# An encoder block on one core: low parts of read-back activations made by GpSimd in place of VectorE

## The chip, the cores and the metric
One core of a Trainium2 chip runs the whole kernel. The metric is the device time in microseconds (us), the median of the runs. The engines are TensorE (PE: matmuls; PEld: its weight loads), VectorE (DVE), ScalarE (ACT), GpSimd (POOL) and SyncE (SP), which here only issues DMAs.

## The reference, cut to what matters
A bidirectional encoder block over 512 tokens with a model width of 2048, in float32: two attention branches merged by gates, then a SwiGLU feed-forward of inner width 5632, then a gated embedding, then a norm. The change lies at the switch inside the feed-forward:

```python
gu = rmsnorm(h, g_ffn[i]) @ w_gate_up[i]
g_, u_ = gu[..., :D_FF], gu[..., D_FF:]
h = h + (jax.nn.silu(g_) * u_) @ w_down[i]
```

## The kernel before, in words
**Precision.** A float32 matmul is made of three fp32r ones: each operand is split in a high part, its copy rounded to fp32r, and a low part, the operand minus the high part. The products are high x high, high x low and low x high. ScalarE makes the high parts, VectorE the low parts, for the weights as they stream in and for the activations.

**Units and products.** The feed-forward is a run of `UNITS` = 68 units, `FF` = 44 for gate and up and 24 for down, each a block of output rows that is computed with seven products in place of eight (a Strassen-Winograd scheme over halves of rows, columns and depth). Units go in pairs, and the products of the two units of a pair alternate: product `order(v, j)` = 14*(v//2) + 2*j + v%2, for j from 0 to 6, so there are 476, numbered 0 to 475. A product is `strassen(v, j)` on TensorE (lines 1197 to 1200 with the high part of the weights, line 1203 with the low part): 8 tiles of depth, 6 in the last generation. Weights of product n sit in slot `ring(n)` of three: ScalarE's `hi(n)` (line 1734, recorded as L1290) waits until TensorE has used product n-3, VectorE's `lo(n)` (line 2554) waits for `hi(n)`, TensorE waits for both. Four weight blocks of a unit (A11, A21, A22, A12) are loaded by SyncE in `block_load` (line 711) into slots of `RAWS`; the other operands of the seven products are sums of them: the first, A21 + A22, is an accumulating DMA that GpSimd issues, `sum_1(v)` (line 3009), after the loads of A21 and A22 of the unit; the others are subtractions of VectorE, `sum_2`, `sum_3`, `sum_4` (lines 2569, 2574, 2579). SyncE loads A22 of unit v after VectorE's `sum_4(v-2)` and `lo(order(v-2, 4))`, and A11 after `lo(order(v-2, 5))`.

**Generations of the down product.** Its activations are 22 row pairs; they are made in the gate-up stage, stored to DRAM (`hidden_store`), and read back as the second operand in three generations: units 44 to 51, 52 to 59 and 60 to 67. For a generation g of 1, 2, 3 there are seven operands x, blocks j = 0 to 6, held in the arena with a high and a low half. SyncE reads a block back with `fill(g, j)` (line 730) into the place of the low half, after TensorE has used the same slot of the generation before. Then each block is split in two parts h: ScalarE's `fill_split` rounds to the high half (L1290, arena<-arena), and `fill_low` (line 2561) subtracts it in place in the low half, 128x1024 values, 128x768 in generation 3. TensorE's first unit of a generation waits before product j for `fill_lo` to reach 14*(g-1) + 2*j + 2 (line 1184), so for both parts of block j.

**Where the fills stand.** `FILLS` (lines 445 to 462) hangs each part on a product number n; ScalarE does the split right after `hi(n)`, VectorE the low part right after `lo(n)`. For blocks 1 to 6 of a generation these are n = f + 10, 11, 13, 14, 16, 17, 19, 20, 22, 23, 25, 26 with f = 294, 350, 406, so 304 to 320, 360 to 376 and 416 to 432; the two parts of block 6 are needed by product f + 26 itself. Blocks 0 are filled ahead: at 170 and 226, at 352 and 353, at 408 and 409. In the same stretches VectorE adds the results of the units from PSUM into `res` (`add`, line 2742: `add_u3`, `add_c11_c12` and others), and up to unit 43 sums, scales and multiplies gate and up.

**Orders written out by hand.** Every engine's program is a fixed list with semaphore waits. On VectorE and ScalarE the loop over q (pairs of units) and t (0 to 13) does product 14*q + t + 2 and, beside it, what a table of `if`s says. GpSimd's list in this stage is `sum_1(v)` for all v and nothing else; it waits for loads most of the time. The first product of unit v waits on TensorE for `add_u3(v-2)`.

The functions that the diff touches and their callers:

Of the kernel before, what the change touches and what calls it, by code (L numbers as in the profile page):

```python
# [25 lines left out]
F32 = mybir.dt.float32  # L26
F32R = mybir.dt.float32r
ALU = mybir.AluOpType
# [52 lines left out]
UNITS = FF + 24  # L81
# [47 lines left out]
def raw_slot(v, i):  # L129

    if v < 2 and i == A12:
        return 8 + v
    return ((0, 7, 2, 4), (1, 5, 3, 6))[v % 2][(i - v // 2) % 4]


def raw_count(v, i):

    before = 0 if v < 2 and i == A12 else 16 * (Z_UNITS // 2)
    return before + (16 * (v // 2) if raw_slot(v, i) in (4, 6) else 16 if v < 2 else 16 * (v // 2 + 1))
# [39 lines left out]
def z_slot(v, i):  # L179

    return ((7, 4, 5, 2), (6, 0, 1, 3))[v % 2][(i - v // 2) % 4]
# [15 lines left out]
def build(nc, xT, pT, gains, tables, mats, w_in, w_z, w_qb, w_kvb, w_a, w_b, w_o, w_gu, w_dn, w_dn6, w_pg, w_pp,  # L197
          outT):
    with ExitStack() as ctx:
# [3 lines left out]
        def sem(name):  # L203
            return ctx.enter_context(nc.semaphore(name))
# [82 lines left out]
        fill_hi, fill_lo, added = sem("fill_hi"), sem("fill_lo"), sem("added")  # L287
# [25 lines left out]
        def sums(norm):  # L313
            return tab[:, 3, :] if norm == 4 else acc[:]
# [46 lines left out]
        def columns(v):  # L361
            return slice(0, pairs(v) * P)

        def ring(n):
            return (1, 0, 2)[n % 3]

        def operand(v, j):

            i = (A11, A21, A22, A12, A21, A12, A22)[j]
            return RAWS[raw_slot(v, i)][:, columns(v)]  # L370

        def x_slot(g, j):
            s, n = (7 * g + j) % 8, 6 if g == 3 else 8
            a = arena[:, 4 * s:4 * s + 4].rearrange("p u t c -> p (u t c)")
            return a[:, 0:n * 512].rearrange("p (t k c) -> p t k c", t=2, k=n)
# [83 lines left out]
        FILLS = {}  # L459
# [4 lines left out]
        def fill_part(g, j, h):  # L464
            n = 3 if g == 3 else 4
            return x_slot(g, j)[:, :, n * h:n * h + n]
# [1514 lines left out]
        def _(dve):  # L1981
            tt = nc.vector.tensor_tensor
# [78 lines left out]
            def head_square_lo(m):  # L2061
                dve.wait_ge(hsq_hi, m + 1)
                hi, lo = sq_parts(m)[:, 0:1, :], sq_parts(m)[:, 1:2, :]
                tt(lo, spare(m)[0], hi, ALU.subtract).then_inc(hsq_lo, 1)
# [252 lines left out]
            def seam_rotate(m, tile, before):  # L2317
                _, r, out = spare(m)
                dve.wait_ge(hnorm, m + 1)
                rotate(m, tile, 0, out, r, HD // 2, 2 * m + 2, before)  # L2320
                dve.wait_ge(roped, m + 1)
# [228 lines left out]
            def lo(n):  # L2550
                v, j = 2 * (n // 14) + n % 2, n % 14 // 2
                dve.wait_ge(s_hi, n + 1)
                s = ring(n)
                tt(S_LO[s][:, columns(v)], operand(v, j), S_HI[s][:, columns(v)], ALU.subtract).then_inc(s_lo, 1)  # L2554
                for part in FILLS.get(n, []):
                    fill_low(*part)

            def fill_low(g, j, h):
                dve.wait_ge(fill_hi, 14 * (g - 1) + 2 * j + h + 1)
                x = fill_part(g, j, h)  # L2560
                tt(x[:, 1], x[:, 1].bitcast(F32), x[:, 0], ALU.subtract).then_inc(fill_lo, 1)  # L2561

            def a_raw(v, i):
                return RAWS[raw_slot(v, i)][:, columns(v)]
# [27 lines left out]
            for g in range(8):  # L2592
# [16 lines left out]
                if g < 7:  # L2609
                    wlo(b + 4, 0)  # L2610
                else:
                    lo(0)
# [6 lines left out]
                if g == 7:  # L2619
                    x_low(14, T2_, SIX, res[:, 0:6, LEFT])  # L2620
                    x_low(15, B22_, SIX, res[:, 8:14, RIGHT])
                    lo(1)
                    x_low(16, T3_, SIX, res[:, 0:6, RIGHT])
# [349 lines left out]
        @block.gpsimd  # L2973
        def _(pool):
            def add_square(s, first, norm, sq):

                out = sums(norm)
                pool.wait_ge(sq_done, s + 1)
                if s == first:
                    if norm:  # L2980
                        pool.wait_ge(rstd_done, norm)
                    nc.gpsimd.tensor_copy(out, sq[:, s % 2, :]).then_inc(acc_done, 1)
                else:
                    pool.wait_ge(acc_done, s)
                    nc.gpsimd.tensor_tensor(out, out, sq[:, s % 2, :], ALU.add).then_inc(acc_done, 1)

            sq_a, sq_b = tmp[:, 2:4, :], tab[:, 0:2, :]
            for v in range(Z_UNITS):
                into, more = z_slot(v, A21), z_slot(v, A22)
                pool.wait_ge(s_in[into], 16 * (v // 2 + 1))  # L2990
                pool.wait_ge(s_in[more], 16 * (v // 2 + 1))
                pool.dma_start(RAWS[into], RAWS[more], accum_op=ALU.add).then_inc(sum_1_in[v % 2], 16)
            for norm, first, end in ((1, 16, 20), (2, 20, 24)):
                for s in range(first, end):
                    add_square(s, first, norm, sq_a)

            for p in range(8):
                pool.wait_ge(emptied, G_MERGE + p + 1)
                if p:
                    pool.wait_ge(mrg_lo, p)  # L3000
                else:
                    pool.wait_ge(gated_a_out[0], 16 * HEADS // 2)
                nc.gpsimd.tensor_tensor(tmp[:, 0:2, :], tmp[:, 2:4, :],
                                        res[:, GATE_IN[p % 2]:GATE_IN[p % 2] + 2, :], ALU.add).then_inc(mrg_sum, 1)
            def sum_1(v):
                into, more = raw_slot(v, A21), raw_slot(v, A22)
                pool.wait_ge(s_in[into], raw_count(v, A21))
                pool.wait_ge(s_in[more], raw_count(v, A22))
                pool.dma_start(RAWS[into][:, columns(v)], RAWS[more][:, columns(v)],  # L3009
                               accum_op=ALU.add).then_inc(sum_1_in[v % 2], 16)  # L3010

            for s in range(24, 38):
                add_square(s, 24, 3, sq_b)
            for v in range(UNITS):
                sum_1(v)
            for g in range(7):
                pool.wait_ge(pg_sig, g + 1)
                pool.wait_ge(emb_normed, 2 * g + 2)
                nc.gpsimd.tensor_tensor(tmp[:, 0:2, :], tmp[:, 0:2, :], emb[:, 2 * g:2 * g + 2, :],
                                        ALU.mult).then_inc(pg_mul, 1)  # L3020
                pool.wait_ge(pg_mul, g + 1)
                if g == 0:
                    pool.wait_ge(u_hi, 42)
                    pool.wait_ge(u_lo, 42)
                    pool.wait_ge(sq_done, 72)
                r = res[:, 2 * g:2 * g + 2, :]
                nc.gpsimd.tensor_tensor(r, r, tmp[:, 0:2, :], ALU.add).then_inc(pg_res, 1)
                for s in (72 + 2 * g, 73 + 2 * g):
                    add_square(s, 72, 6, sq_b)
# [117 lines left out]
```

## Time and profile before

| | us |
|---|---|
| median of 3 runs (2654.67 to 2655.56) | 2655.09 |
| the profiled execution's own time | 2658.29 |
| its span, first to last instruction | 2656.5 |
| TensorE matmuls busy | 2632.9 |
| VectorE busy | 2020.0 |
| ScalarE busy | 1286.2 |
| GpSimd busy | 179.1 |
| mean granted clock of TensorE, share of full speed | 0.998 |

"Busy" is the union of an engine's instructions; the matmuls are pipelined, so one of 256 columns is recorded with 0.28 us while the next starts 0.12 us later. Times in the trace are counted from the start of the span. The feed-forward runs from about 1125 to 2445 us.

### The profile page before, as it was taken

How to read it: one execution, taken by the hardware profiler on the slowest of the kernel's cores; microseconds unless marked ns; L12 is line 12 of the kernel's file. 1: busy time of each engine (PE TensorE's matmuls, PEld its weight loads, DVE VectorE, ACT ScalarE, POOL GpSimd, SP SyncE). 2: the span in 40 equal slices, each digit the busy share in tenths (PEclk: the TensorE clock that was granted, in tenths of full speed). 3: DMA queues.
4: the chain of work that ended last, by engine and by line, in shares of the span. 5: the costliest groups of instructions: out<-in, count | busy, mean ns of one | idle time of the engine just before them, and what ended most of it. 6: DMA issues, size and time to landing. Idle time of an engine off the chain costs nothing. (4 is left out here: it accounts for less than half of the span.)

```text
span 2656.5 us, 37937 instructions
## 1 busy us (share of the span) xinstructions
PE 2632.9 (99%) x14980; PEld 2309.0 (87%) x14980; DVE 2020.0 (76%) x2310; ACT 1286.2 (48%) x1612; POOL 179.1 (7%) x140
## 2 busy tenths in 40 slices
PE   9999999999999999999999999999999999999997
PEld 7989888888888888898888888888899898999887
DVE  7888767655565433488998999899899898888745
ACT  7545455434445233454554555554554453444543
POOL 0000000010000111100000000000000000000052
PEclk9999999999999999999999999999999999999999
DMA  7455323223333554446545555554666664643332
GB/s 247 139 160 163 127 87 95 79 88 112 107 94 108 182 208 124 146 126 180 165 143 177 172 153 167 175 151 151 177 210 216 190 224 126 208 137 106 94 103 96
DMA packets 137055, 392.75 MB, mean 148 GB/s; under 512 B 11584, under 2 KB 43456, under 8 KB 134336
## 3 DMA queue, kind: packets, MB, share of 16 engines
q1 hardware_dynamic: 121168, 342.27, 37.7%
q0 software_dynamic: 11232, 39.85, 8.5%
q10 hardware_dynamic: 4496, 8.44, 0.8%
q8 instruction: 109, 1.79, 0.3%
q14 instruction: 50, 0.41, 0.0%
HBM read 304.26 MB, written 46.40 MB: 132 GB/s over the span
## 5 line engine op out<-in xcount | busy, mean ns | idle before, releaser
L1290 ACT ACTIVATE w_hi<-raw 128x1024 fp32r<-128x1024 f32 (+1 forms) x539 | 563.3, 1046 | 756.8 <-PE ps L1203 408.3
L827 PE MATMUL ps<-arena,w_hi 128*128 128x512 f32 x2704 | 647.6, 391 | 1.3 <-DVE arena L2059 1.1
L827 PEld LDWEIGHTS ps<-arena,w_hi 128*128 128x128 f32 x2704 | 505.3, 188 | 109.9 <-issue 4.9
L1197 PE MATMUL ps<-arena,w_hi 128*128 128x512 f32 x1792 | 448.8, 392 | 0.5 <-DVE res L2742 0.5
L2554 DVE TENSOR_TENSOR w_lo<-raw,w_hi 128x1024 fp32r<-128x1024 f32 (+1 forms) x315 | 375.0, 1191 | 80.0 <-ACT w_hi L1290 78.3
L2005 DVE TENSOR_TENSOR w_lo<-raw,w_hi 128x1024 fp32r<-128x1024 f32 x172 | 219.3, 1275 | 233.3 <-ACT w_hi L1290 231.6
L1197 PEld LDWEIGHTS ps<-arena,w_hi 128*128 128x128 f32 x1792 | 322.3, 189 | 58.3 <-DVE res L2742 0.7
L1203 PEld LDWEIGHTS ps<-arena,w_lo 128*128 128x128 f32 x2468 | 332.3, 191 | 17.6
L1203 PE MATMUL ps<-arena,w_lo 128*128 128x256 f32 x2468 | 346.4, 282 | 0.0
L832 PE MATMUL ps<-arena,w_lo 128*128 128x512 f32 x1352 | 334.3, 389 | 0.0
L1290 ACT ACTIVATE hi<-raw 128x1024 fp32r<-128x1024 f32 (+1 forms) x183 | 190.4, 1041 | 250.8 <-PE ps L1203 208.2
L832 PEld LDWEIGHTS ps<-arena,w_lo 128*128 128x128 f32 x1352 | 253.8, 188 | 52.7
L1197 PE MATMUL ps<-arena,hi 128*128 128x512 f32 x896 | 224.4, 392 | 0.0
L2554 DVE TENSOR_TENSOR lo<-raw,hi 128x1024 fp32r<-128x1024 f32 (+1 forms) x157 | 187.1, 1192 | 46.7 <-ACT hi L1290 46.1
L1197 PEld LDWEIGHTS ps<-arena,hi 128*128 128x128 f32 x896 | 161.1, 189 | 28.8
L1203 PEld LDWEIGHTS ps<-arena,lo 128*128 128x128 f32 x1228 | 166.0, 191 | 8.7
L1203 PE MATMUL ps<-arena,lo 128*128 128x256 f32 x1228 | 172.9, 283 | 0.0
L1199 PE MATMUL ps<-arena,w_hi 128*128 128x256 f32 x676 | 166.9, 284 | 0.2 <-ACT res L1290 0.2
L1200 PE MATMUL ps<-arena,w_hi 128*128 128x256 f32 x676 | 166.7, 284 | 0.0
L3009 POOL DMA_DIRECT2D raw<-raw x68 | 59.1, 869 | 1224.0 <-DMA raw<-w_gu 785.8
L1199 PEld LDWEIGHTS ps<-arena,w_hi 128*128 128x128 f32 x676 | 130.3, 193 | 0.5 <-ACT res L1290 0.4
L1200 PEld LDWEIGHTS ps<-arena,w_hi 128*128 128x128 f32 x676 | 130.2, 193 | 0.1
(272 smaller groups left out, 3358.6 us busy)
## 6 DMA issues: line engine op xcount, KB each, us to landing
raw<-w_gu SPq DMA_DIRECT2D x174, 512.0 KB, 4.0
raw<-raw POOLq DMA_DIRECT2D x70, 512.0 KB, 7.9
raw<-w_in SPq DMA_DIRECT2D x68, 512.0 KB, 3.4
raw<-w_dn SPq DMA_DIRECT2D x64, 512.0 KB, 4.5
hid<-res SPq DMA_DIRECT2D x22, 1024.0 KB, 5.0
raw<-w_z SPq DMA_DIRECT2D x40, 512.0 KB, 5.0
raw<-w_o SPq DMA_DIRECT2D x32, 512.0 KB, 3.7
raw<-w_pg SPq DMA_DIRECT2D x32, 512.0 KB, 3.6
```

What stands on the lines that cost most here:

```text
L827: mm(ps[:, bank + t, :], w_hi[:, s, t, k], x[:, part, :], start=first and k == 0 and part == 0, stop=False)
L832: i = mm(ps[:, bank + t, :], w_lo[:, s, t, k], x[:, 0, :], start=False, stop=last and k == len(xs) - 1)
L1197: mm(parts, w, x[:, :, k], start=fresh and k == 0, stop=False, skip_group_check=not fresh)
L1199: mm(out, w, x[:, 0, k], start=fresh and k == 0, stop=False, skip_group_check=not fresh)
L1200: mm(out, w, x[:, 1, k], start=False, stop=False, skip_group_check=not fresh)
L1203: i = mm(out, lo[:, k * P:k * P + P], x[:, 0, k], start=False, stop=k == pairs(v) - 1, skip_group_check=not fresh)
L1290: return nc.scalar.activation(out, in_, ACT.Copy, scale=scale)
L2005: tt(w_lo[:, j % HL], raw[:, j], w_hi[:, j % HL], ALU.subtract).then_inc(w_lo_done, 1)
L2554: tt(S_LO[s][:, columns(v)], operand(v, j), S_HI[s][:, columns(v)], ALU.subtract).then_inc(s_lo, 1)
L3009: pool.dma_start(RAWS[into][:, columns(v)], RAWS[more][:, columns(v)], accum_op=ALU.add).then_inc(sum_1_in[v % 2], 16)
```

## The change
VectorE's `fill_low` and its call in `lo(n)` are taken out. The same function, with the same wait and the same semaphore, stands in GpSimd's program, and GpSimd's plain loop of `sum_1` becomes a loop over pairs of units in which the fills of products 14*q + 2 to 14*q + 15 stand around the two transfers of the next pair: places 2 to 9, then the even unit's transfer, place 10, the odd unit's transfer, places 11 to 15. `FILLS`, ScalarE, TensorE and SyncE are as before.

```diff
@@ VectorE
                 tt(S_LO[s][:, columns(v)], operand(v, j), S_HI[s][:, columns(v)], ALU.subtract).then_inc(s_lo, 1)
-                for part in FILLS.get(n, []):
-                    fill_low(*part)
-
-            def fill_low(g, j, h):
-                dve.wait_ge(fill_hi, 14 * (g - 1) + 2 * j + h + 1)
-                x = fill_part(g, j, h)
-                tt(x[:, 1], x[:, 1].bitcast(F32), x[:, 0], ALU.subtract).then_inc(fill_lo, 1)
@@ GpSimd
-            for v in range(UNITS):
-                sum_1(v)
+            def fill_low(g, j, h):
+                pool.wait_ge(fill_hi, 14 * (g - 1) + 2 * j + h + 1)
+                x = fill_part(g, j, h)
+                nc.gpsimd.tensor_tensor(x[:, 1], x[:, 1].bitcast(F32), x[:, 0], ALU.subtract).then_inc(fill_lo, 1)
+
+            def fill_lows(first, end):
+                for n in range(first, end):
+                    for part in FILLS.get(n, []):
+                        fill_low(*part)
+
+            sum_1(0)
+            sum_1(1)
+            for q in range(UNITS // 2):
+                fill_lows(14 * q + 2, 14 * q + 10)
+                if 2 * q + 2 < UNITS:
+                    sum_1(2 * q + 2)
+                fill_lows(14 * q + 10, 14 * q + 11)
+                if 2 * q + 3 < UNITS:
+                    sum_1(2 * q + 3)
+                fill_lows(14 * q + 11, 14 * q + 16)
```

## Rows read from the trace of the kernel before

**Rows 1.** Page, part 1: busy us, share of the span, instructions.
```profile
PE 2632.9 (99%) x14980; PEld 2309.0 (87%) x14980; DVE 2020.0 (76%) x2310; ACT 1286.2 (48%) x1612; POOL 179.1 (7%) x140
```

**Rows 2.** Waits of TensorE, whole span: us in total, times, longest.
```profile
PE ps L1199 <- DVE res L2742: 2.3, 1, 2.3
...
PE ps L1199 <- issue: 1.0, 1, 1.0
...
PE ps L1197 <- DVE res L2742: 0.5, 1, 0.5
```

**Rows 3.** Timeline of VectorE: products 317, 320 (its fill), 373, 429 (start, us).
```profile
2022.63 1.22 DVE L2554 TENSOR_TENSOR lo<-raw,hi 128x1024 fp32r<-128x1024 f32 x1
2023.76 1.22 DVE L2561 TENSOR_TENSOR arena<-arena 128x1024 fp32r<-128x1024 f32 x1
...
2031.58 1.22 DVE L2561 TENSOR_TENSOR arena<-arena 128x1024 fp32r<-128x1024 f32 x1
...
2182.85 1.22 DVE L2554 TENSOR_TENSOR w_lo<-raw,w_hi 128x1024 fp32r<-128x1024 f32 x1
...
2335.94 0.95 DVE L2554 TENSOR_TENSOR w_lo<-raw,w_hi 128x768 fp32r<-128x768 f32 x1
```

**Rows 4.** Timeline of TensorE: first matmuls of products 320, 376 and 432.
```profile
2032.90 0.36 PE L1199 MATMUL ps<-arena,hi 128*128 128x256 f32 x1 [1.02 <-issue]
...
2192.58 0.28 PE L1199 MATMUL ps<-arena,w_hi 128*128 128x256 f32 x1
...
2342.79 0.28 PE L1199 MATMUL ps<-arena,w_hi 128*128 128x256 f32 x1
```

**Rows 5.** Timeline of ScalarE and VectorE before TensorE's wait at 2349.5.
```profile
2346.31 0.84 ACT L1290 ACTIVATE hi<-raw 128x768 fp32r<-128x768 f32 x1 [4.57 <-DMA raw<-w_dn]
...
2348.07 1.41 DVE L2742 TENSOR_TENSOR res<-ps,res 128x512 f32<-128x512 f32 x2
```

**Rows 6.** Windows: length, busy (instructions) of PE, PEld, DVE, ACT, POOL; clock; DMA.
```profile
2350.00:2360.00 10.00, 10.00 (x74) 10.00 (x73) 7.40 (x11) 3.06 (x4) 0.00 (x0) 0.83 0.18 61
...
2360.00:2370.00 10.00, 10.00 (x86) 10.00 (x85) 9.69 (x13) 5.26 (x7) 0.00 (x0) 1.00 0.21 64
```

**Rows 7.** The same columns, three stretches with nine fills each.
```profile
1981.11:2022.63 41.52, 41.52 (x348) 41.44 (x347) 41.20 (x45) 26.64 (x30) 1.22 (x2) 1.00 0.76 262
2142.09:2182.85 40.76, 40.76 (x342) 40.76 (x341) 37.19 (x38) 24.20 (x24) 1.37 (x2) 1.00 0.64 214
2300.95:2335.94 34.99, 34.99 (x294) 34.99 (x293) 31.02 (x38) 19.81 (x24) 0.91 (x2) 1.00 0.57 179
```

**Rows 8.** Line 3003, GpSimd's additions ahead of w_o: ns min/median/max.
```profile
L3003 POOL TENSOR_TENSOR tmp<-tmp,res x8: 2391/2391/3300, 890.0 to 962.9; 128x1024 f32<-128x1024 f32 x8
```

**Rows 9.** Timeline of the tail, VectorE and GpSimd together.
```profile
2526.86 1.22 DVE L2017 TENSOR_TENSOR tmp<-ps,rstd 128x1024 f32<-128x1024 f32 x1
...
2527.55 1.30 POOL L2985 TENSOR_TENSOR acc<-acc,tab 128x512 f32<-128x512 f32 x1
...
2530.21 2.41 POOL L3019 TENSOR_TENSOR tmp<-tmp,emb 128x1024 f32<-128x1024 f32 x1 [1.35 <-DVE emb L2891]
2531.15 2.54 DVE L2005 TENSOR_TENSOR w_lo<-raw,w_hi 128x1024 fp32r<-128x1024 f32 x1 [1.09 <-ACT w_hi L1290]
2532.70 3.25 POOL L3027 TENSOR_TENSOR res<-res,tmp 128x1024 f32<-128x1024 f32 x1
```

**Rows 10.** Windows, VectorE's instructions on tile ps, first two stretches: busy (instructions), clock, DMA.
```profile
1981.11:2022.63 41.52, 4.77 (x8) 1.00 0.76 262
2142.09:2182.85 40.76, 5.70 (x10) 1.00 0.64 214
```

**Rows 11.** Timeline of GpSimd: accumulating transfers of units 47, 55 and 63.
```profile
2030.34 0.87 POOL L3009 DMA_DIRECT2D raw<-raw  x1 [6.26 <-DMA raw<-w_dn]
...
2189.20 0.86 POOL L3009 DMA_DIRECT2D raw<-raw  x1 [4.28 <-DMA raw<-w_dn]
...
2340.87 0.86 POOL L3009 DMA_DIRECT2D raw<-raw  x1 [2.78 <-DMA raw<-w_dn]
```

## The prediction, made before the change was run

> **What bounds the kernel now.** I read the busy times first: TensorE's matmuls cover 99% of the span of 2656.5 us, VectorE is at 76%, GpSimd at 7% [rows 1]. So nothing gets faster unless TensorE waits less, and anything gets slower that makes it wait. The chain of waits, TensorE's own part, comes next: in the stage of the edit (the switches between the gate-up product and the three generations of the down product) it waits three times: 1.0 us at 2032.9, 0.5 us a little later, and 2.3 us at 2349.5 [rows 2]. The 1.0 us is named "issue", but VectorE's low fill, the very instruction that moves, runs from 2031.58 for 1.22 us and TensorE goes on at 2032.90 [rows 3, 4]: it is the last fill of generation 1 that ends the wait. The 2.3 us end with an addition of VectorE that stood behind a weight block whose load was waited for 4.57 us [rows 5]; that load is issued once VectorE has made a low part, so a late VectorE is behind that wait too. After it the granted clock is 0.83 over ten microseconds, between the levels 2.4 and 1.2 GHz, and 74 matmuls start in place of about 86 (the stretch after it) [rows 6]: 12 x 0.12 us, 1.4 us more. The whole stake of the faster side is thus 1.0 + 0.5 + 2.3 + 1.4 = 5.2 us, 0.2% of the time.
>
> Why VectorE is late there is seen in three stretches, each from the first of a generation's fills to the start of the low part of the tenth product of the generation's first fourteen (317, 373, 429): it is busy 41.20 of 41.52, 37.19 of 40.76 and 31.02 of 34.99 us [rows 7], with nine fills in each. The relief is aimed at the right engine.
>
> **What is removed.** 42 subtractions on VectorE, 28 of 1024 columns and 14 of 768. In a back-to-back row one takes 1.13 us of its time (2022.63 to 2023.76) [rows 3]; for 768 columns I take 3/4 of that, 0.85. Two of the 42 (generation 1, block 0) and the four of blocks 0 of the others lie where VectorE has gaps: I cost them at nothing: the cover is those gaps and the ring of three slots that lets the low parts run ahead of TensorE; without it each would cost the 1.3 us by which the new hold is longer.
>
> **What is added.** The same subtraction on GpSimd. No row shows it in fp32r; the nearest is GpSimd's addition of 128x1024 f32 from two SBUF tiles, 2.39 us at least and in the middle, 3.30 at most [rows 8]. I take 2.39 us (1.8 for 768 columns, 3/4), upper bound 3.30; the lower bound is VectorE's own 1.13, since a rounding output could not make it faster than the faster engine.
>
> The decisive price is another. In the tail both engines work on SBUF at once, and there they don't share: GpSimd's multiply starts 2530.21 and takes 2.41, to 2532.62; VectorE's low part, normally 1.22, starts at 2531.15 and takes 2.54, to 2533.69, which is GpSimd's end plus 1.07. GpSimd's next addition, begun at 2532.70, then takes 3.25 in place of 2.39 [rows 9]. One waits for the other to end. An instruction of VectorE with an input in PSUM passes freely: L2017 (from ps and rstd) takes its 1.22 us at 2526.86, and GpSimd's addition that begins under it its 1.30 [rows 9]. The Trainium skill says the same and speaks against this change (SBUF — State Buffer, "Who interferes with whom": a VectorE instruction with two SBUF inputs and a GpSimd one that reads SBUF exclude each other for a whole instruction, while one SBUF input is free); by that rule moving a fill takes 2.39 us from VectorE in place of 1.13, not zero, and the trace agrees with its 2.54 us.
>
> So each move costs VectorE time. Nine fills per stretch: 9 x 2.39 = 21.5 us blocked, 9 x 1.13 = 10.2 us freed, +11.3 (generation 3: 16.2 - 7.7 = +8.5). Off that goes work that passes freely, VectorE's instructions on PSUM, 4.77 and 5.70 us [rows 10] and as much again in the third,, of which I take half since they come up at any point of a hold, and VectorE's idle time, 0.3, 3.6 and 4.0 us [rows 7]. VectorE reaches products 317, 373 and 429 later by
> 11.3 - 2.4 - 0.3 = 8.6; 11.3 - 2.85 - 3.6 = 4.9; 8.5 - 2.85 - 4.0 = 1.7 us.
>
> **The queue of GpSimd.** It is in order. The fills of its places 11 and 12 (block 6, both halves) stand behind the accumulating transfer of the odd unit, and this one waits for a weight block whose load SyncE issues only after VectorE's low part of product 317 (373, 429). From the start of that low part to the transfer's issue it is 2030.34 - 2022.63 = 7.7, 2189.20 - 2182.85 = 6.35 and 2340.87 - 2335.94 = 4.9 us [rows 3, 11]. The issue takes 0.87; then come two fills, 4.8 us (3.6), and 0.1 us to TensorE, which needs both for product 320 (376, 432). It would start it at
> 2022.63 + 8.6 + 7.7 + 0.9 + 4.8 + 0.1 = 2044.7, against 2032.90 [rows 4]: +11.8, less the 0.5 us wait right after it, +11.3;
> 2182.85 + 4.9 + 6.35 + 0.9 + 4.8 + 0.1 = 2199.9, against 2192.58: +7.3;
> 2335.94 + 1.7 + 4.9 + 0.9 + 3.6 + 0.1 = 2347.1, against 2342.79: +4.3, less the 2.3 us that were waited one unit on (its load lands meanwhile): +2.0.
> The other queued work: the even unit's transfer stands behind fill place 9 and goes out some microseconds late, but its user, ScalarE's high part of the unit's second product, comes six products on; SyncE's waits are on VectorE and are in the lateness above. ScalarE's split is untouched.
>
> Sum 20.6 us. **The clock:** before, a wait of 2.3 us brought a dip worth 1.4 and one of 1.0 none [rows 2, 6]; now three generations wait long, two dips more, 2.8 us. Together 23.4 us. The profiled execution took 2658.3 us, 3.2 above the median of the runs, so this is 2681.7 for it and 2655.1 + 23.4 = 2678 for the median. Bounds: all PSUM work beside the holds takes 2.4 + 2.85 + 1.7 = 7 off (2671); none of it beside adds 8, and 0.9 us of waiting (3.30 against 2.39) in each of the last six fills 5 (2692).
>
> **Rivals.**
> A, as above, both the blocked VectorE and the transfer ahead of the last fills. 0.66, 2678, own range 2668 to 2694.
> B, VectorE isn't made late, because holds fall into its gaps and on PSUM work, and only the order on GpSimd costs: transfers at their present times, plus 0.9 + 4.8 + 0.1 (0.9 + 3.6 + 0.1): 2036.1, 2195.0, 2345.5, so 3.2 - 0.5, 2.4 and 2.7 - 2.3, 5.5 us, and one more dip: 2662. For it: generations 2 and 3 have gaps; against: 1 has none. 0.12.
> C, faster: the fp32r subtraction doesn't exclude VectorE, or hardly. Then VectorE gains 10 us per stretch, low parts keep their lead, loads and transfers go out some 4 us earlier, the two last fills are ready in time, and all 5.2 us go: 2650. It decides if VectorE's low parts stay at 1.22 us beside a GpSimd fill. Against it stand 2.54 and 3.25 [rows 9]. 0.09.
> D, GpSimd fares worse: with VectorE back to back it gets the port late each time. If each of the first ten fills in a generation waits the 0.9 us and none of the PSUM work helps, that is 8 + 5 + 3 x 4 us above A (half of the waits on the path): 2703. No row shows a GpSimd instruction against VectorE instructions that follow each other without a gap. 0.09.
> E, the lead hides it and waits only change places: within 0.2%. 0.04.
>
> **How the numbers follow.** What a measurement of this kernel can tell from no change is about 0.2% (5.3 us). Faster is C, 0.09; same E and a corner of B, 0.05; slower A, D and nearly all of B, 0.86. The range runs from just under B to D, 2660 to 2704; left out are C, E and the far ends, under 0.2.
>
> **What would show it.** Right: VectorE's low parts of 1024 columns at 1.9 us and more in these stretches and 1.22 elsewhere; GpSimd fills of 2.4 to 3.4 us; TensorE's waits on GpSimd's fills near 2033, 2200 and 2360, over 4 us each, the first the longest; the odd transfer just ahead of the two last fills; granted clock under 1 behind them. Wrong: VectorE's instructions unstretched (C), or waits of 2 to 3 us only, with VectorE's low parts on time (B). A wait that ends on an addition of VectorE rather than on a fill would tell that the lateness, not the queue, is the term that counts.

## The result, and the profile after

The changed kernel takes 2692.11 us (median of 4 runs, 2688.3 to 2692.75) against 2654.97 us of the kernel before: ratio 1.0136, 95% interval 1.0124 to 1.0148. It is 37.1 us slower. The profiled execution took 2692.14 us with a span of 2690.2; against the profiled execution before, which lay 3.3 us above its median, it is 33.9 us longer. The sums below are against that one. Two of the ten runs of e1_none below (2867.61 and 5639.47 us) and one of the ten of e3_queue_only (6127.92) were slow ones; the medians of the others are 2651.53 and 2651.52 us.

Page of the changed kernel, part 1, busy us, share of the span, instructions:

```profile
PE 2645.6 (98%) x14980; PEld 2319.7 (86%) x14980; DVE 2046.7 (76%) x2268; ACT 1285.9 (48%) x1612; POOL 288.6 (11%) x182
```

VectorE has 42 instructions fewer than in [rows 1] and is busy 27 us longer: those that are left were stretched by more than the 42 had taken. TensorE's waits over the whole span, where [rows 2] had 2.3, 1.0 and 0.5 us in this stage:

```profile
PE ps L1199 <- issue: 8.7, 3, 3.1
PE ps L1203 <- DVE w_lo L2554: 7.5, 6, 2.2
PE ps L1203 <- DVE lo L2554: 4.6, 3, 2.5
...
PE ps L1199 <- DVE res L2735: 2.3, 1, 2.3
PE ps L1199 <- DVE res L2689: 1.9, 1, 1.9
```

Two kinds make 20.8 of the 25.0 us; the last two lines are additions of VectorE that came late. Line 1203 is the last third of a product, the one that needs VectorE's low part: nine times it came too late (12.1 us), which happened nowhere in the kernel before. And three times TensorE stands before a product with the name "issue": these are the last fills of the three generations, on GpSimd now. Timeline of GpSimd, then of TensorE at the end of each generation (start, us):

```profile
2041.19 0.87 POOL L3002 DMA_DIRECT2D raw<-raw  x1 [6.37 <-DMA raw<-w_dn]
2041.75 5.01 POOL L3010 TENSOR_TENSOR arena<-arena 128x1024 fp32r<-128x1024 f32 x2
```

```profile
2046.86 0.55 PE L1199 MATMUL ps<-arena,hi 128*128 128x256 f32 x1 [2.90 <-issue]
...
2219.01 0.35 PE L1199 MATMUL ps<-arena,w_hi 128*128 128x256 f32 x1 [2.75 <-issue]
...
2378.16 0.55 PE L1199 MATMUL ps<-arena,w_hi 128*128 128x256 f32 x1 [3.09 <-issue]
```

The odd unit's transfer goes out, the two fills stand behind it, and TensorE starts product 320 at 2046.86, 0.1 us after the second fill ends (2041.75 + 5.01). Products 376 and 432 are the other two rows, again 0.1 us after a last fill. Now the price itself. Timeline of GpSimd at the first fills of generation 1, and of VectorE beside it:

```profile
1981.69 2.49 POOL L3010 TENSOR_TENSOR arena<-arena 128x1024 fp32r<-128x1024 f32 x1 [0.53 <-ACT arena L1290]
1984.30 0.88 POOL L3002 DMA_DIRECT2D raw<-raw  x1
1984.91 2.71 POOL L3010 TENSOR_TENSOR arena<-arena 128x1024 fp32r<-128x1024 f32 x1
```

```profile
1980.69 1.23 DVE L2554 TENSOR_TENSOR w_lo<-raw,w_hi 128x1024 fp32r<-128x1024 f32 x1 [0.45 <-ACT w_hi L1290]
1981.84 2.90 DVE L2682 TENSOR_TENSOR res<-res,rstd 128x512 f32<-128x512 f32 x1
1984.67 3.51 DVE L2696 TENSOR_TENSOR res<-res 128x512 f32<-128x512 f32 x1
1988.11 1.21 DVE L2554 TENSOR_TENSOR lo<-raw,hi 128x1024 fp32r<-128x1024 f32 x1
```

Two instructions of 512 columns, 0.69 us long where GpSimd rests, take 2.90 and 3.51 us: each ends 0.6 us after a fill of GpSimd (1984.18 and 1987.62). The windows of [rows 7], taken at the same instructions (length, busy and instructions of PE, PEld, DVE, ACT, POOL, clock, DMA):

```profile
1980.71:2034.25 53.54, 47.03 (x366) 45.93 (x365) 51.98 (x37) 27.48 (x32) 30.33 (x13) 0.94 0.61 202
2158.41:2208.03 49.62, 44.22 (x352) 43.61 (x351) 46.91 (x31) 24.06 (x25) 31.84 (x12) 0.97 0.54 182
2328.94:2368.79 39.85, 36.65 (x301) 36.04 (x301) 31.80 (x30) 20.07 (x25) 23.32 (x12) 1.00 0.50 156
```

The stretches became 12.0, 8.9 and 4.9 us longer, with 8, 7 and 8 instructions of VectorE fewer in them.

**The clock.** Between consecutive matmuls of this stage, spaces are 0.12 us (256 columns) and 0.23 (512) at full clock. Of all that is longer, I count spaces up to 2.3 times as long as a slow clock, and longer ones as waits. Waits sum to 28.2 us after and 4.2 before, slow spaces to 12.5 after and 1.9 before: 24.0 + 10.6 = 34.6 us, the whole 33.9 us within the count's error. Windows show such a place, the same columns:

```profile
1998.40:2005.10 6.70, 4.82 (x23) 4.52 (x23) 6.70 (x8) 2.00 (x2) 3.02 (x1) 0.50 1.03 383
2000.00:2010.00 10.00, 8.53 (x57) 8.53 (x58) 8.47 (x8) 4.51 (x5) 4.63 (x2) 0.74 0.96 352
2010.00:2020.00 10.00, 10.00 (x86) 10.00 (x85) 10.00 (x7) 4.27 (x5) 6.56 (x3) 1.00 0.35 107
```

A wait of 2.2 us ends at 1997.9, and from 1998.4 to 2005.1, with a second wait of about 2 us inside, the granted clock is 0.50, the lower level of 1.2 GHz; in the ten microseconds from 2010 on it is back at 1.00.

### The profile page after: what moved, and what is told of

Read it like the earlier page. It is cut to its first block and busy times, and to the rows that moved or that the text cites. A ratio compares the mean times of both kernels' runs of the same rounds, so it can differ in the third digit from the quotient of the medians.

```text
span 2690.2 us, 37937 instructions
## 1 busy us (share of the span) xinstructions
PE 2645.6 (98%) x14980; PEld 2319.7 (86%) x14980; DVE 2046.7 (76%) x2268; ACT 1285.9 (48%) x1612; POOL 288.6 (11%) x182
## 5 line engine op out<-in xcount | busy, mean ns | idle before, releaser
L2554 DVE TENSOR_TENSOR w_lo<-raw,w_hi 128x1024 fp32r<-128x1024 f32 (+1 forms) x315 | 396.6, 1259 | 85.1 <-ACT w_hi L1290 83.2
L2554 DVE TENSOR_TENSOR lo<-raw,hi 128x1024 fp32r<-128x1024 f32 (+1 forms) x157 | 197.6, 1258 | 46.2 <-ACT hi L1290 45.6
L1199 PE MATMUL ps<-arena,w_hi 128*128 128x256 f32 x676 | 171.4, 289 | 8.3 <-issue 5.8
L1200 PE MATMUL ps<-arena,w_hi 128*128 128x256 f32 x676 | 170.9, 288 | 0.0
```

The lines of the kernel that those rows point to most:

```text
L1199: mm(out, w, x[:, 0, k], start=fresh and k == 0, stop=False, skip_group_check=not fresh)
L1200: mm(out, w, x[:, 1, k], start=False, stop=False, skip_group_check=not fresh)
```

## The experiments

Theory P: the two engines exclude each other at SBUF, so moved fills block VectorE for longer than they relieved it, and its late low parts hold up TensorE. Rival Q: it is GpSimd's queue and its slower instruction that TensorE waits for. All times are medians. The runs stand on three chips; the kernel before, run beside them on each, took 2654.81 to 2654.99 us, so that they can be set against each other.

**Relief alone (e1_none).** Nobody makes the low halves of the read-back activations: TensorE does as many matmuls as before, on the unsplit values, so the result lacks that correction.

```diff
-                    pe.wait_ge(fill_lo, 14 * (g - 1) + 2 * j + 2)
+                    pe.wait_ge(fill_hi, 14 * (g - 1) + 2 * j + 2)
...
-                for part in FILLS.get(n, []):
-                    fill_low(*part)
```

> Nobody makes the low halves of the read-back blocks: TensorE waits for ScalarE's split alone and multiplies the unsplit values in the low half (the low halves of these activations are left out). It is the relief of VectorE without any load on GpSimd. Both theories (P: the two engines exclude each other at SBUF, so VectorE is blocked; Q: only the in-order queue of GpSimd and its slower instruction make TensorE wait) expect the waits at products 320, 322 and 434 to go: 2650, from 2648 to 2653. If it stays at 2655, the waits of the kernel before were never VectorE's.

Measured 2651.65 us, ratio 0.9988 (0.9977 to 0.9998): 3.2 us faster, and the trace has no wait of TensorE in this stage. So this is about the most that a relief of VectorE can bring here, and the base against which the others are set.

**Blocking alone (e2_block_only, e9_block_two_tiles).** In e2 GpSimd ran two subtractions on the tile acc at each fill's place and TensorE waited for none of it (the low halves left out as before).

```diff
-                x = fill_part(g, j, h)
-                nc.gpsimd.tensor_tensor(x[:, 1], x[:, 1].bitcast(F32), x[:, 0], ALU.subtract).then_inc(fill_lo, 1)
+                c = acc[:, 0:384 if g == 3 else 512]
+                nc.gpsimd.tensor_tensor(c, c, c, ALU.subtract).then_inc(fill_mid, 1)
...
+                pool.wait_ge(fill_mid, len(fills_made))
+                nc.gpsimd.tensor_tensor(c, c, c, ALU.subtract).then_inc(fill_lo, 1)
```

> As e1_none, but GpSimd runs, at each place of a fill and after the same wait for ScalarE's split, two subtractions of half the width each on the unused tile acc (about 2 x 1.3 us), and nobody on TensorE's path waits for them: the port is held about as long as by a fill, GpSimd's queue keeps its order and length, but TensorE never waits for a fill. P expects VectorE's low parts stretched to 1.9 to 2.8 us and TensorE waiting for them: 2665 to 2680. Q expects 2650 to 2653, as e1_none.

Measured 2662.01 us, 10.4 above e1 but under the range that was given for P, and above that of Q. Its trace showed a flaw of the experiment: with one tile as both inputs an undisturbed subtraction of 512 columns took 1.04 us, not the 1.29 that additions of two tiles take elsewhere. It was repeated with a second tile (256 of its columns, read twice).

```diff
-                nc.gpsimd.tensor_tensor(c, c, c, ALU.subtract)
+                d = cm[:].rearrange("p t c -> p (t c)")[:, None, 0:k].broadcast_to([P, 2, k])
+                nc.gpsimd.tensor_tensor(c, c, d, ALU.subtract)
```

> e2_block_only with one thing mended: there both inputs were the same tile, and such a subtraction of 512 columns took 1.04 us in place of 1.29, so the port was held too short. Now the second input is another tile (cm, repeated). As there the low halves are left out and TensorE waits for none of it. If VectorE being blocked is nearly all of the loss, 2672 to 2682 (e4_order lost 29 us against e1_none). If the loss is mostly TensorE's own waiting for the fills, 2662 to 2667, little above e2_block_only.

Measured 2678.77 us (2676.82 to 2680.06): 27.1 us above e1. TensorE's waits there, none of them on GpSimd, since it waits for none of it:

```profile
PE ps L1204 <- DVE w_lo L2555: 5.6, 7, 1.3
PE ps L1204 <- DVE lo L2555: 5.1, 4, 2.5
PE ps L1200 <- DVE res L2690: 3.5, 1, 3.5
PE ps L1200 <- DVE res L2736: 2.1, 2, 1.2
PE ps L1198 <- DVE res L2736: 1.7, 1, 1.7
```

Line 1204 is 1203 of the others. With nobody waiting for GpSimd, its subtractions in SBUF alone make VectorE late. The two runs also say how steep it is: in e2 an undisturbed pair of subtractions is 0.5 us shorter (0.4 in generation 3), some 19 us over 42 fills, and e2 is 17 us faster. At this margin nearly every microsecond of hold arrives at TensorE, though the first ones cost less: e9's whole loss is 27 us, for pairs of 2.6 us (2.0 in generation 3). How the loss runs between these points was not measured.

**Queue alone (e3_queue_only).** GpSimd writes zeros twice in place of the subtraction, TensorE waits for them; it reads nothing from SBUF. The low halves are zero, so their products, which are still computed, add nothing.

```diff
-                nc.gpsimd.tensor_tensor(x[:, 1], x[:, 1].bitcast(F32), x[:, 0], ALU.subtract).then_inc(fill_lo, 1)
+                y = x[:, 1].bitcast(F32)
+                nc.gpsimd.memset(y, 0.0).then_inc(fill_mid, 1)
...
+                pool.wait_ge(fill_mid, len(fills_made))
+                nc.gpsimd.memset(y, 0.0).then_inc(fill_lo, 1)
```

> The changed kernel with GpSimd's subtraction replaced by two fills with zero, which read nothing from SBUF, in the same queue places and with TensorE waiting for them (the low halves of these activations are left out, they are zero). If they take about 2 us together, the queue and its order are as in the changed kernel while VectorE is not blocked. P expects VectorE's instructions at their normal 1.22 us, loads and transfers early, and TensorE waiting little: 2651 to 2662. Q expects most of the loss to stay: 2678 to 2692.

Measured 2651.55 us, e1's time to 0.1 us. The groups of GpSimd from 1500 to 2480 us and one line of VectorE's low parts (ns min/median/max):

```profile
L3014 POOL MEMSET arena<- 128x1024 f32 x28 | 27.5, 984 | 81.7 <-ACT arena L1291 81.7
L3017 POOL MEMSET arena<- 128x1024 f32 x28 | 26.8, 956 | 1.6
```

```profile
L2555 DVE TENSOR_TENSOR w_lo<-raw,w_hi x315: 947/1225/1228, 1124.7 to 2429.9; 128x1024 fp32r<-128x1024 f32 x139, 128x768 fp32r<-128x768 f32 x19
```

1.9 us of GpSimd in the same places of the same queue, and not one of 315 low parts of VectorE is above 1.23 us. The zeros are 0.5 us shorter than a fill of 2.40 us, but that doesn't save Q: the last ones end at 2029.66, 2188.51 and 2339.46, and products 320, 376 and 432 start at 2031.12, 2189.97 and 2340.18, so 0.7 us and more were to spare. The odd units' transfers went out at 2024.06, 2182.18 and 2335.58, 5 to 7 us earlier than in [rows 11]. The queue and a fill's latency cost nothing as long as VectorE isn't blocked. (The Trainium skill, SBUF — State Buffer, "Who interferes with whom", says that a GpSimd instruction that only writes doesn't contend with VectorE's second input; the runs agree.)

**Blocking and waiting (e10_block_and_wait).** e9 with TensorE's wait on `fill_lo` put back, one line.

```diff
-                    pe.wait_ge(fill_hi, 14 * (g - 1) + 2 * j + 2)
+                    pe.wait_ge(fill_lo, 14 * (g - 1) + 2 * j + 2)
```

> As e9_block_two_tiles, but TensorE waits before the products for GpSimd's subtractions as it does for the fills in the changed kernel: that wait is the one difference. If blocking and waiting together are the whole change, this comes to the changed kernel's time, 2686 to 2694, and the difference to e9 is what TensorE's own wait for GpSimd costs, 8 to 14 us by e4_order; if it comes out well below, something in the real fills (in fp32r, in the arena) costs more than the held port and the queue.

Measured 2695.86 us (2695.54 to 2697.23), 17.1 above e9, where 8 to 14 had been expected, and 3.8 above the changed kernel, whose fills are one instruction each and not two with a wait between; that this makes the 3.8 us was not shown. So the change is rebuilt from its parts, the slower clock included in each: relief -3.2, blocking +27.1, waiting for fills that the contention made late +17.1, 41.0 in all against 37.1; waiting without blocking 0.

**The order on GpSimd (e4_order, e6_early_gpsimd).** e4 puts the odd transfer behind the last two fills.

```diff
-                fill_lows(14 * q + 10, 14 * q + 11)
+                fill_lows(14 * q + 10, 14 * q + 13)
                 if 2 * q + 3 < UNITS:
                     sum_1(2 * q + 3)
-                fill_lows(14 * q + 11, 14 * q + 16)
+                fill_lows(14 * q + 13, 14 * q + 16)
```

> The changed kernel with the odd unit's accumulating transfer put behind the fills of places 11 and 12 in place of ahead of them; nothing is left out. P expects the waits on the last fills of each generation (3 us and more at products 320, 376 and 432) to shrink by some 3 to 5 us each, with VectorE's blocking as it was: 2678 to 2685. Q expects nearly all the loss to go: 2655 to 2662.

Measured 2680.82 us (2680.42 to 2681.24): 11.3 less than the changed kernel. The queue order is worth that much, but only on top of the blocking (e3). The waits named "issue" fell from 8.7 to 3.1 us, those on VectorE's low parts stayed:

```profile
PE ps L1203 <- DVE w_lo L2554: 6.8, 6, 2.0
PE ps L1203 <- DVE lo L2554: 4.6, 3, 2.5
PE ps L1199 <- issue: 3.1, 3, 1.5
```

e6 also hangs the fills three products earlier:

```diff
-                    n = first + 3 * j + 7 + h
+                    n = first + 3 * j + 4 + h
```

> e4_order with all fills of blocks 1 to 6 hung three products earlier, nothing left out: the same holds of the port, but no fill is needed by the product at which it is made. If half of the loss of e4_order (26 us) is TensorE waiting for fills that come late, 2662 to 2672; if it is VectorE's low parts that are late, the holds only move: 2674 to 2682.

Measured 2682.66 us (2680.78 to 2683.15). No gain, and 0.7 us over the slower of the two ranges: TensorE's waits on VectorE's low parts are 14.7 us here and 11.4 in e4, so the holds only moved.

**One long hold or two short (e5_split).**

```diff
+                for a, b in ((0, k), (k, x.shape[2])):
+                    i = nc.gpsimd.tensor_tensor(x[:, 1, a:b], x[:, 1, a:b].bitcast(F32), x[:, 0, a:b], ALU.subtract)
+                i.then_inc(fill_lo, 1)
```

> The changed kernel with each fill on GpSimd cut in two subtractions of half the width (512 or 384 columns), nothing left out. The port is held as long in sum, but in pieces of about 1.3 us. e2_block_only, with such pieces, lost only 10 us against e1_none, the changed kernel 40. If the length of one hold is what hurts (VectorE loses up to a whole 2.4 us at a time and GpSimd waits up to a whole 1.2 us before it), the time falls to 2672 to 2684. If it is the sum of the holds and TensorE's waits on the fills, it stays at 2688 to 2695 or rises a little.

Measured 2689.71 us (2687.92 to 2692.97), the changed kernel's time within the spread: the length of a single hold is not what hurts. The cut gains nothing in sum either: GpSimd's pieces of 512 columns took 1.82 us on the mean, where an undisturbed addition of that width takes 1.29. (In generation 3 the cut falls at 256 and 512 columns, not at 384.)

**One generation (e8_gen2_gpsimd).** Only generation 2's fills on GpSimd.

> Only generation 2's fills on GpSimd, the others on VectorE as before, nothing left out. The trace of the changed kernel lays 12 of its 34 us to this generation. If the generations are independent, 2655 + 12 = 2667, from 2664 to 2669, with no wait of TensorE at generation 1 beyond those of before.

Measured 2668.12 us (2665.38 to 2668.93), +13.1, where the changed kernel's trace gives generation 2 11.7 us: its stretch starts 2158.41 - 2142.09 = 16.3 us later than before, generation 3's 2328.94 - 2300.95 = 28.0 us. TensorE's wait at product 320 is 1.02 us, as before. For this generation the loss is its own and doesn't depend on the others; the other two were not run alone.

**Fills earlier on VectorE (e7_early_vector).** The kernel before with the shift of e6.

> The kernel before with the fills of blocks 1 to 6 hung three products earlier, on VectorE, nothing left out. e1_none shows that all waits of this stage together are worth 3.2 us. If they come from the crowding of VectorE at the end of each stretch, the earlier fills use its gaps ahead of it and 1 to 3 us go: 2652 to 2654. If VectorE's work is too much in any order: 2655, within 0.7 us.

Measured 2654.78 us (11 runs), ratio 1.000 (0.9991 to 1.0009). No version here beats the kernel before and computes the whole; e1 shows that at most 3.2 us are to be had from VectorE's load in this stage.

## Why the prediction was right, and where its sizes were off

Forecast A, slower by 23.4 us to 2678 (range 2660 to 2704, A's own 2668 to 2694), came true in kind and within both ranges: measured 2692, +37.1, 1.6 times the sum. That it meets A's upper bound of 2692 is luck: the bound came from VectorE's PSUM work finding no room beside the holds and from fills that wait 0.9 us, and the sum was short mostly elsewhere. By its steps:

**What bounds it.** Right. All waits and slow spaces of this stage sum to 6.1 us in the profiled execution of before, and e1 removed them. The stake was put at 5.2 us; the medians give 3.2; the profiled execution lay 3.3 us above its median.

**GpSimd's price.** Right as a bound, a little low as a mean: taken 2.39 with 3.30 as bound; the 28 fills of 1024 columns took 2.40 to 3.39 us, 2.93 on the mean, those of 768 from 1.91 to 2.84.

**The exclusion.** Right, and shown by e3 against e10: the same places in the queue and the same waits, without and with reads of SBUF, 2651.55 and 2695.86 us. Instructions with an input in PSUM pass freely here too: in the first two stretches VectorE's are busy 4.76 and 5.67 us, against 4.77 and 5.70 in [rows 10]. Rival C (no exclusion) would have been about e3's time. B priced the queue without blocking at +5.5 us; e3 shows 0, because B kept the transfers at their old times, while a relieved VectorE lets them go 5 to 7 us earlier. D, GpSimd starved at 2703, didn't come: no fill waited for more than one instruction of VectorE.

**VectorE's lateness.** Right as a mechanism, and the term of the sum that was mis-sized most on VectorE's side. Foretold were 8.6, 4.9 and 1.7 us, 15.2 in all; the stretches grew by 12.0, 8.9 and 4.9, 25.8 in all, 10.6 us more. That this equals the miss against the profiled execution (33.9 against 23.4) is in part chance: the queue came 2 us cheaper, the clock behind the stretches, from the starts of products 320, 376 and 432 on, 2.4 us dearer (5.2 for 2.8). Two counts in it failed.

The first is "off that goes VectorE's idle time, 0.3, 3.6 and 4.0 us". Idle time is length less busy in the windows: before 0.3, 3.6 and 4.0 us, after 1.6, 2.7 and 8.1. So 7.9 us were to be used up, and the sum grew by 4.5. Generation 3 shows why. Its stretch cut after 20 us, before and after, the columns of [rows 7], and what ScalarE waited for in the first part after:

```profile
2300.95:2320.95 20.00, 20.00 (x169) 20.00 (x168) 16.04 (x19) 10.95 (x13) 0.91 (x2) 1.00 0.83 256
2320.95:2335.94 14.99, 14.99 (x127) 14.99 (x126) 14.99 (x20) 8.87 (x11) 0.00 (x0) 1.00 0.23 78
```

```profile
2328.94:2348.94 20.00, 20.00 (x169) 20.00 (x169) 11.95 (x14) 10.93 (x13) 11.70 (x8) 1.00 0.86 267
2348.94:2368.79 19.85, 16.65 (x135) 16.04 (x134) 19.85 (x17) 9.14 (x12) 11.62 (x5) 1.00 0.15 44
```

```profile
ACT w_hi L1290 <- PE ps L1203: 3.8, 4, 1.1
ACT hi L1290 <- PE ps L1203: 3.0, 2, 1.8
ACT w_hi L1290 <- DMA raw<-w_dn: 2.1, 1, 2.1
```

All of VectorE's idle time lies in the first part, before as after. There TensorE runs without a wait at full clock, ScalarE mostly waits until it has used a slot of the ring, and VectorE waits for ScalarE: it can't get further ahead. The holds in this part cost TensorE nothing, and the time that the moved fills freed became more idle time, 8.1 us in place of 4.0. In the second part VectorE has no gap, before or after, and it grew from 14.99 to 19.85 us, the whole 4.9. I had taken idle time from anywhere in a stretch off the holds at its end. In generations 1 and 2 part of the idle time is a consequence of the lateness itself: 1.5 us at 2005.9 and 1.4 us after 2176.3 stand behind waits of TensorE, since ScalarE's next high part waits for TensorE, and VectorE for ScalarE.

The second is the number of holds, nine. The windows after have ten fills in each stretch: the tenth, of place 317, stood behind product 317's low part on VectorE, and on GpSimd it is free to run ahead of it. GpSimd and VectorE in generation 1:

```profile
2028.65 3.37 POOL L3010 TENSOR_TENSOR arena<-arena 128x1024 fp32r<-128x1024 f32 x1
```

```profile
2029.70 3.41 DVE L2572 TENSOR_TENSOR raw<-raw 128x1024 f32<-128x1024 f32 x1
```

The tenth fills stretch instructions of VectorE by 2.2, 1.7 and 1.7 us. In generations 1 and 2 that is about what busy time grew by beyond the forecast (10.8 and 9.7 us for 8.9 and 8.5); in generation 3 it grew by 0.8 only for 5.7, since about half of the holds fell into the part with the idle time.

**The queue of GpSimd.** Right to about a microsecond: from the tenth product's low part to the transfer 7.0, 5.3 and 4.8 us (foretold 7.7, 6.35, 4.9), from the transfer to TensorE's start 5.7, 5.7 and 4.6 (5.8, 5.8, 4.6). What the text didn't give is its worth by itself: e9 and e10 put TensorE's waiting for fills at 17 of the 44 us that blocking and waiting cost together, e4 the order in the queue at 11.

**The waits of before.** Right: the 0.5 us and the 2.3 us are gone; after product 432 TensorE waits for no engine in this stage. The 2.3 us on an addition of VectorE in the list after is another wait, at 2176.3 in generation 2.

**The clock.** Seen from TensorE, this is the term that was mis-sized most. Foretold 2.8 us; slow spaces grew by 10.6 us, while the waits grew by 24.0 for the 20.6 foretold. (About 4 of the 10.6 us lie inside the stretches and so in the lateness above: the two views overlap and don't add.) Before, one wait of 2.3 us had brought 1.4 us; I allowed for two dips more. After, eleven waits of 1 us and more stand in the stage, and the clock is at 1.2 GHz in six places, some 31 us in all, where it was in one for under 4 us. The step that failed is one dip for each generation's long wait: the waits on late low parts bring dips as well, as at 1998.

**What would show it.** Low parts stretched, fills of 2.4 to 3.4 us, waits near 2047, 2219 and 2378 (foretold 2033, 2200 and 2360, and over 4 us each; they are 2.8 to 3.1; TensorE had by then been held up by late low parts). The sign named for "lateness, not the queue, is the term that counts" was a wait that ends on VectorE: it is 16.3 of the 25.0 us of the waits shown above.

## What to carry to other kernels

Before moving an elementwise instruction with two SBUF inputs from VectorE to GpSimd, look in the trace for a place where both work at once: if VectorE's instruction ends a fixed time after GpSimd's, the move costs VectorE up to GpSimd's duration (2.4 us) and frees its own (1.1 us). Idle time of an engine inside a loop of three engines isn't a store to draw on: split the stretch, and count it as cover only for what falls into it, not for the crowded part behind it. Count the instructions in the new engine's own order too; one that stood behind another on the old engine may run ahead of it on the new. And expect short waits that recur to cost clock as well: here 24 us of waits brought 10.6 us more. A rebuild from parts (no work, port held but nobody waits, waiting but port free, both) tells contention and latency apart in four runs.

## What the runs showed of the hardware that was not expected

VectorE can be passed over by GpSimd more than once. Timeline of GpSimd and of VectorE at the end of generation 2 in the changed kernel:

```profile
2213.33 0.86 POOL L3002 DMA_DIRECT2D raw<-raw  x1 [1.82 <-DMA raw<-w_dn]
2213.89 5.01 POOL L3010 TENSOR_TENSOR arena<-arena 128x1024 fp32r<-128x1024 f32 x2
```

```profile
2214.57 5.43 DVE L2554 TENSOR_TENSOR lo<-raw,hi 128x1024 fp32r<-128x1024 f32 x1 [1.28 <-ACT hi L1290]
```

A low part of 1.22 us took 5.43: it waited through both fills, which follow each other without a gap, and ended 1.1 us after the second. It happens at the last two fills of all three generations (in generation 1 an instruction takes 5.70 us from 2041.62, in generation 3 one takes 5.00 from 2373.89). It isn't the rule: of the two fills from 1990.33 on, which also follow each other without a gap, the first delays VectorE's instruction at 1990.98 to 1993.88 and the second the next one, to 1996.68. What decides between the two was not looked into. The other way round no fill took more than 3.39 us, 1.0 above its least, though VectorE was back to back: GpSimd waited for less than one of VectorE's instructions of 1.22 us. And a GpSimd subtraction of 512 columns whose two inputs are the same tile takes 1.04 us, with two tiles 1.29.
